# Experts of a two-block network: eleven places for 2 MB weight pieces instead of nine, tokens gathered per group, residual summed in PSUM

## The reference, cut to what matters

```
def ec_moe(x, w_router, w_e_gate, w_e_up, w_e_down):        # x: 1 x 256 x 1024
    cap = CAP_FACTOR * T // N_EXPERTS                       # 32 tokens for each expert
    aff = softmax(x @ w_router)                             # 256 x 16
    g, idx = top_k(aff.transpose(0, 2, 1), cap)
    xs = x[idx]                                             # 16 experts x 32 tokens x 1024
    a = einsum('becd,edf->becf', xs, w_e_gate)              # 16 weights of 1024 x 1024
    u = einsum('becd,edf->becf', xs, w_e_up)
    y = einsum('becf,efd->becd', silu(a) * u, w_e_down) * g
    return zeros(T, D).at[idx].add(y)

x = x + g2 * ec_moe(modulate(rmsnorm(x, norm2), sh2, sc2), ...)
return rmsnorm(x, final_norm)
```

## Time and profile before

| | us |
|---|---|
| median of three runs | 2156.92 |
| lowest, highest | 2155.39, 2157.17 |
| profiled execution, its own time | 2155.87 |
| its span, first to last instruction | 2154.10 |
| PE busy | 1896.1 |
| VectorE busy | 774.6 |
| ACT busy | 523.3 |
| last expert piece used by PE | 2138.10 to 2141.57 |

### The profile page before, as it was taken

One profiled execution on the slowest core, in us unless ns is written; L12 is line 12 of the kernel. 1 busy time (PEld: TensorE's weight loads), 2 busy tenths in 40 slices (PEclk: granted clock), 3 DMA queues, 4 the chain that ended last, 5 costly groups with the idle time before them and its releaser, 6 DMA issues.

```text
span 2154.1 us, 26066 instructions
## 1 busy us (share of the span) xinstructions
PE 1896.1 (88%) x11262; PEld 1434.2 (67%) x11262; DVE 774.6 (36%) x1312; ACT 523.3 (24%) x780; POOL 0.2 (0%) x4
## 2 busy tenths in 40 slices
PE   6999999899998999999999999998999886565555
PEld 5799876799997898766799999545788522111111
DVE  3442332645634433243555675423344300000001
ACT  2201121144431101121244453433352210000000
POOL 0000000000000000000000000000000000000000
PEclk9999999999999999999999999999999998877877
DMA  6221331444442221543644431211025899999996
GB/s 252 98 98 64 152 157 66 189 181 171 173 160 78 90 106 59 210 169 148 242 188 166 177 132 64 78 59 40 1 79 207 349 427 427 428 427 427 427 428 295
DMA packets 30643, 414.13 MB, mean 192 GB/s; under 512 B 3392, under 2 KB 3648, under 8 KB 4288
## 3 DMA queue, kind: packets, MB, share of 16 engines
q1 hardware_dynamic: 29808, 408.69, 47.5%
q10 hardware_dynamic: 720, 3.78, 0.4%
HBM read 411.41 MB, written 1.05 MB: 191 GB/s over the span
## 4 chain that ended last, share of the span: by engine, by line
PE 62%; DMA 18%; DVE 12%; ACT 7%; issue 1%; DVEq 0%; ACTq 0%
PE ps L219 46%; PE ps L751 7%; DMA high<-in_w_e_down_dram 7%; DMA high<-in_w_e_up_dram 6%; DVE rarena L178 4%; ACT rarena L213 4%; DMA high<-in_w_e_gate_dram 4%; PE ps L1141 3%; DVE low L178 3%; PE ps L1503 3%; DVE high L178 2%; ACT high L213 1%; ACT low L213 1%; DVE high L188 1%; PE ps L747 1%
## 5 line engine op out<-in xcount | busy, mean ns | idle before, releaser
L219 PE MATMUL ps<-high,ring 128*128 128x256 f32 (+1 forms) x2016 | 481.9, 390 | 6.3 <-DMA ring<-in_w_in_dram 4.4
L219 PE MATMUL ps<-rarena 128*128 128x256 f32 (+1 forms) x3648 | 457.7, 287 | 7.4 <-DVE rarena L178 7.4
L219 PEld LDWEIGHTS ps<-rarena 128*128 128x128 f32 x3648 | 446.7, 191 | 16.7 <-DVE rarena L178 10.4
L219 PEld LDWEIGHTS ps<-high,ring 128*128 128x128 f32 x2016 | 375.3, 192 | 79.8 <-issue 19.9
L213 ACT ACTIVATE high<-ps 128x512 f32<-128x512 f32 (+2 forms) x210 | 103.2, 492 | 707.3 <-PE ps L1503 275.5
L1503 PE MATMUL ps<-high,low 128*32 128x512 f32 x1040 | 157.1, 733 | 97.5 <-DMA high<-in_w_e_down_dram 35.2
L178 DVE TENSOR_TENSOR rarena<-ring,rarena 128x2048 fp32r<-128x2048 f32 x76 | 167.3, 2201 | 137.5 <-ACT rarena L213 135.8
L213 ACT ACTIVATE rarena<-ring 128x2048 fp32r<-128x2048 f32 x76 | 140.0, 1842 | 149.2 <-DMA ring<-in_w_ffn_up_dram 84.9
L1503 PEld LDWEIGHTS ps<-high,low 128*32 128x32 f32 x1040 | 30.8, 123 | 213.8 <-issue 56.1
L178 DVE TENSOR_TENSOR high<-high,ps 128x512 f32<-128x512 f32 x52 | 35.8, 688 | 314.8 <-PE ps L1503 257.1
L751 PE MATMUL ps<-high 128*128 128x128 f32 (+6 forms) x1024 | 128.8, 298 | 15.3 <-DVE high L178 10.7
(11 more groups left out here) (147 smaller groups left out, 1352.2 us busy)
## 6 DMA issues: line engine op xcount, KB each, us to landing
ring<-in_w_in_dram SPq DMA_DIRECT2D x36, 2048.0 KB, 7.4
ring<-in_w_ffn_up_dram SPq DMA_DIRECT2D x22, 2048.0 KB, 7.5
high<-in_w_e_gate_dram SPq DMA_DIRECT2D x22, 2048.0 KB, 40.7
high<-in_w_e_up_dram SPq DMA_DIRECT2D x22, 2048.0 KB, 41.3
high<-in_w_e_down_dram SPq DMA_DIRECT2D x21, 2048.0 KB, 41.4
ring<-in_w_mod_dram SPq DMA_DIRECT2D x12, 2048.0 KB, 9.3
ring<-in_w_e_down_dram SPq DMA_DIRECT2D x11, 2048.0 KB, 40.6
ring<-in_w_e_gate_dram SPq DMA_DIRECT2D x10, 2048.0 KB, 40.5
```

What stands on the lines that cost most here:

```text
L219: ins = self.e.matmul(out, l, r, start=first and i == 0, stop=end and i == n - 1)
```

## The change

Two more slots (`LOWER`, 9 and 10) are cut from the upper end of the lower arena. In the order of the pieces they stand behind slots 3 and 4 and ahead of the two ring slots that hold the output projection. To make room, buffers of the expert stage are shared or moved: `h2t` lies on `h2` (so ACT waits for the transposes that read the part it writes over), `xs` holds one group's tokens, `hid`, `hT` and `y` are one buffer, the squares use four places instead of eight, `SG` lies over constants that are no longer needed, `fb` over `Sm`, the output over `x`. Tokens are gathered per group, in two batches between the first down steps of the group before. The residual is added by PE: 16 matmuls of `x` with the identity into the combine's open PSUM sums. Squares and the last scaling read PSUM. Turned weights and the row `g2b` are made between the first group's up steps, the row `fb` between the last group's down steps.

```diff
@@ -23,6 +23,7 @@
+LOWER = 2
@@ -287,7 +288,7 @@
-        s_slot = [sem(f"s_slot{i}_landed") for i in range(NSLOT + MORE)]
+        s_slot = [sem(f"s_slot{i}_landed") for i in range(NSLOT + MORE + LOWER)]
@@ -302,6 +303,7 @@
+        slots += [low[:, LOW - (i + 1) * SLOT:LOW - i * SLOT] for i in range(LOWER)]
@@ -535,30 +537,32 @@
-        E.h2t = alloc(2, 1024)
-        E.xs = alloc(8, 512)
-        E.Sm, E.SG = alloc(2, 512), alloc(2, 512)
+        E.h2t = halves(flat(E.h2))
+        E.xs = alloc(8, 128)
+        E.sq = flat(E.xs).rearrange("p (a n) -> p a n", a=4)
...
-        assert place["top"] <= LOW
+        assert place["top"] <= LOW - LOWER * SLOT
...
-        E.SGT = alloc(4, 256)
+        E.Sm = alloc(2, 512)
...
-        E.mx, E.ixu, E.ixf = (E.hid[:, 0, 32 * i:32 * i + 32] for i in range(3))
...
-        E.sq = flat(E.xs)[:, 0:2048].rearrange("p (a n) -> p a n", a=8)
...
-        E.at = flat(E.xs)[:, 2304:2816].rearrange("p (a n) -> p a n", a=2)
-        E.hT = flat(E.Sm).rearrange("p (a n) -> p a n", a=8)
-        E.y4 = halves(flat(E.h2))
-        E.ot = E.y4
-        E.xt = E.h2t
-        E.g2b, E.fb = flat(E.SG), flat(E.bi)
+        top16 = flat(E.hid)
+        E.at = halves(top16[:, 0:512])
+        E.mx, E.ixu, E.ixf = (top16[:, 512 + 32 * i:544 + 32 * i] for i in range(3))
+        E.SG = halves(low[:, top_2 - 256:top_2 + 768])
+        assert coff["e16"][1] >= 768
+        E.SGT = flat(E.bi).rearrange("p (a n) -> p a n", a=4)
+        E.hT = flat(E.hid).rearrange("p (a n) -> p a n", a=8)
+        E.y = flat(E.hid)
+        E.g2b, E.fb = flat(E.SG), flat(E.Sm)
+        E.ot = halves(flat(x))
@@ -705,7 +709,7 @@
-            order = ring_[:1] + [5, 6, 7, 8] + [3, 4] + ring_[1:]
+            order = ring_[:1] + [5, 6, 7, 8] + [3, 4] + [9, 10] + ring_[1:]
@@ -1428,8 +1432,8 @@
-            for t in (1, 0):
-                for hh in range(2):
+            for hh in range(2):
+                for t in range(2):
@@ -1441,7 +1445,7 @@
-            PE.wait_ge("h211", "h210", "h201", "h200")
+            PE.wait_ge("h211")
@@ -1458,10 +1462,13 @@
-            def rest_of_tokens(i):
+            def tokens_of(g_, h):
...
-                b = take_bank(6 + i % 2, f"xs{i}.ps", f"xs{i}")
-                gathered(b[:, 0:384], i, 128, 512).then_inc(*PE(f"xs{i}.ps"))
+                b = take_bank(h, f"xg{g_}{h}.ps", f"xg{g_}{h}")
+                for i in range(4):
+                    ins = gathered(b[:, 128 * i:128 * i + 128], 4 * h + i, 128 * g_, 128 * g_ + 128)
+                ins.then_inc(*PE(f"xg{g_}{h}.ps"))
@@ -1470,29 +1477,28 @@
-                b = take_bank(6 + hh, f"xt{t}{hh}.ps", f"xt{t}{hh}")
-                transposes([(b[:, 128 * i:128 * i + 128], x[:, 4 * hh + i, 128 * t:128 * t + 128])
-                            for i in range(4)]).then_inc(*PE(f"xt{t}{hh}.ps"))
-            def rows(hh):
-                for bank, name, column in ((4, "g2b", lambda i: mod[:, 40 + i, 0:1]),
-                                           (6, "fb", lambda i: pc("final_norm_2", i))):
-                    b = take_bank(bank + hh, f"{name}{hh}.ps", f"{name}{hh}")
-                    for i in range(4):
-                        ins = one(b[:, 128 * i:128 * i + 128], column(4 * hh + i).to_broadcast([128, 128]), ident)
-                    ins.then_inc(*PE(f"{name}{hh}.ps"))
-            between = {("gate", i): (lambda i=i: first_tokens(i + 2)) for i in range(6)}
-            between["gate", 6] = slots_of_tokens
-            for i in range(8):
-                between["up", i] = lambda i=i: rest_of_tokens(i)
-            for t in range(2):
-                between["down", t] = lambda t=t: turned_weights(t)
-                for hh in range(2):
-                    between["down", 2 + 2 * t + hh] = lambda t=t, hh=hh: residual(t, hh)
-            for hh in range(2):
-                between["down", 6 + hh] = lambda hh=hh: rows(hh)
+                for i in range(4):
+                    PE.e.matmul(banks[4 + 2 * t + hh][:, 128 * i:128 * i + 128], x[:, 4 * hh + i, 128 * t:128 * t + 128],
+                                ident, start=False, stop=False)
+            def row(name, bank, hh, column):
+                b = take_bank(bank, f"{name}{hh}.ps", f"{name}{hh}")
+                for i in range(4):
+                    ins = one(b[:, 128 * i:128 * i + 128], column(4 * hh + i).to_broadcast([128, 128]), ident)
+                ins.then_inc(*PE(f"{name}{hh}.ps"))
+            between = {(0, "gate", i): (lambda i=i: first_tokens(i + 2)) for i in range(6)}
+            between[0, "gate", 6] = slots_of_tokens
+            for z in range(2):
+                between[0, "up", 4 + z] = lambda z=z: turned_weights(z)
+                between[0, "up", 6 + z] = lambda z=z: row("g2b", 6 + z, z, lambda i: mod[:, 40 + i, 0:1])
+                for g_ in range(3):
+                    between[g_, "down", z] = lambda g_=g_, z=z: tokens_of(g_ + 1, z)
+                between[3, "down", z] = lambda z=z: row("fb", z, z, lambda i: pc("final_norm_2", i))
+                for t in range(2):
+                    between[1, "gate", 1 + 2 * t + z] = lambda t=t, z=z: residual(t, z)
@@ -1503,8 +1509,8 @@
-                    if g_ == 0 and (nm, k) in between:
-                        between[nm, k]()
+                    if (g_, nm, k) in between:
+                        between[g_, nm, k]()
@@ -1516,16 +1522,14 @@
-                                          E.y4[:, g_ % 2, 512 * ch:512 * ch + 512], start=g_ == 0, stop=g_ == 3)
+                                          E.y[:, 512 * ch:512 * ch + 512], start=g_ == 0, stop=g_ == 3)
...
-                if g_ < 3:
-                    ins.then_inc(*PE(f"comb{g_}"))
...
-                mine = lambda k, e_: E.xs[:, k, 128 * g_ + 32 * e_:128 * g_ + 32 * e_ + 32]
-                if g_ == 1:
-                    PE.wait_ge("xs7")
+                mine = lambda k, e_: E.xs[:, k, 32 * e_:32 * e_ + 32]
+                if g_:
+                    PE.wait_ge(f"xg{g_}1")
@@ -1956,43 +1960,45 @@
-            for t in (1, 0):
+            for t in range(2):
...
-                    A.wait_ge(f"h2{t}{hh}.ps")
+                    A.wait_ge("h210.ps" if (t, hh) == (0, 0) else "h201.ps" if t == 0 else "h211.ps")
...
-            def slots_out(name, i, lo, b):
-                A.wait_ge(f"{name}{i}.ps")
-                A.act(E.xs[:, i, lo:lo + b.shape[1]], b, ACT.Identity, bias=mod[:, 24 + i, 0:1]).then_inc(*A(f"{name}{i}"))
+            def slots_out(i, z):
+                return A.act(E.xs[:, i, :], z, ACT.Identity, bias=mod[:, 24 + i, 0:1])
...
-                slots_out("xs0", i, 0, ps(f"xs0{i}.ps")[:, 0:128])
+                A.wait_ge(f"xs0{i}.ps")
+                slots_out(i, ps(f"xs0{i}.ps")[:, 0:128]).then_inc(*A(f"xs0{i}"))
...
-                A.wait_ge(f"e{g_}gate7.used", f"et{g_ - 1}1.ps" if g_ else "bi2")
+                A.wait_ge(f"e{g_}gate7.used", "bi2")
...
-                    for i in range(8):
-                        slots_out("xs", i, 128, ps(f"xs{i}.ps")[:, 0:384])
...
-                    for t in range(2):
-                        for hh in range(2):
-                            A.wait_ge(f"xt{t}{hh}.ps")
-                            take_copy(E.xt[:, t, 512 * hh:512 * hh + 512], ps(f"xt{t}{hh}.ps")).then_inc(
-                                *A(f"xt{t}{hh}"))
...
-                        for name, dst in (("g2b", E.g2b), ("fb", E.fb)):
-                            A.wait_ge(f"{name}{hh}.ps")
-                            take_copy(dst[:, 512 * hh:512 * hh + 512], ps(f"{name}{hh}.ps")).then_inc(*A(f"{name}{hh}"))
+                        A.wait_ge(f"g2b{hh}.ps")
+                        take_copy(E.g2b[:, 512 * hh:512 * hh + 512], ps(f"g2b{hh}.ps")).then_inc(*A(f"g2b{hh}"))
+                for h in range(2):
+                    if g_ < 3:
+                        A.wait_ge(f"xg{g_ + 1}{h}.ps")
+                        for i in range(4):
+                            ins = slots_out(4 * h + i, ps(f"xg{g_ + 1}{h}.ps")[:, 128 * i:128 * i + 128])
+                            ins.then_inc(*(A(f"xg{g_ + 1}{h}") if i == 3 else A()))
+                    else:
+                        A.wait_ge(f"fb{h}.ps")
+                        take_copy(E.fb[:, 512 * h:512 * h + 512], ps(f"fb{h}.ps")).then_inc(*A(f"fb{h}"))
...
-                    A.wait_ge(f"os{t}{ch}", "et31.ps")
-                    A.act(E.hid[:, ch, :], E.xt[:, t, 512 * ch:512 * ch + 512], ACT.Square,
+                    A.wait_ge(f"acc{t}{ch}")
+                    A.act(flat(E.xs)[:, 512 * ch:512 * ch + 512], banks[4 + 2 * t + ch][:, :], ACT.Square,
@@ -2651,9 +2657,10 @@
-                    V.tt(E.sq[:, i, :], x[:, i, :], x[:, i, :], mul).then_inc(*V())
+                    sq = E.sq[:, i if i < 4 else 1, :]
+                    V.tt(sq, x[:, i, :], x[:, i, :], mul).then_inc(*V())
...
-                        V.tt(E.sq[:, 0, :], E.sq[:, 0, :], E.sq[:, i, :], add).then_inc(*V(f"sq{i}.x"))
```

(19 more changed lines are left out.)

## The result

| | before | changed |
|---|---|---|
| median of five runs, us | 2155.39 | 2144.35 |
| lowest, highest | 2153.98, 2157.17 | 2142.51, 2147.18 |
| profiled execution, us | 2155.87 | 2142.51 |
| its span | 2154.10 | 2140.70 |

The ratio is 0.9949, with a 95% interval of 0.9936 to 0.9963: 11.0 us less (8.0 to 13.8). Forecast was 2146.0 in a range of 2142.6 to 2149.8. Two of the five runs before came after the forecast and lowered that median by 1.5 us, and with it the footing; the difference that was forecast was 10.9 us.

What follows compares the result with a forecast made beforehand. One stream of 96 weight loads sets the end, by its start, its holes and what follows its last landing. Hole 9.7 plus tail 1.2 is 10.9 us off the 2156.92 median: 2146.0, range 2142.6 to 2149.8.

Steps and rivals of the forecast that it cites:

- the hole: Dry stretch of the weight-load stream from 1696, before load 9's bytes: 10.0 us, of which two more slots win 9.7.
- the tail: Work after the last landing, combine to last scaling: without the four adds 1.2 us less, bounds 0.8 and 1.6.
- The rest of the hole: Gap left ahead of load 11, which waits for the first expert step: about 0.3 us instead of 10.0.
- The moved evacuations: ACT's four evacuations of transposed tokens ahead of the first expert step: end 0.75 us later, costed at nothing under 2.0 cover.
- The gathers per group: Tokens gathered in two batches ahead of each of groups 1 to 3, 2.8 us a batch: zero cost, hidden by the stream.
- The first step comes late: Rival, chance 0.10: moved evacuations or PE code fetches delay the first expert step; three us late give 2149.0.
- The hole stays: Rival, chance 0.05: queue takes no tenth and eleventh load ahead, or lower slots come no earlier; only tail won, 2155.7.
- the stream gets slower: Rival, chance 0.03: eleven loads in flight lengthen each load; at 5.10 us for 4.90 the time is 2165.2.
- The tail at half clock: Rival, chance 0.10: the combine after the last expert step runs at half clock, 6.7 us for 3.70, giving 2149.0.
- fixed cost of about 2.0 us of a transfer: Alternative rule for load 11: all 2.0 us ahead of its bytes, starting them at 1707.6, gain 9.2; forecast used 1.46.

Runs made afterwards that it cites:

- e4_late: Changed kernel with four idle 128x512 matmuls ahead of the first expert step; median 2147.95 us, ratio 0.9971 to the kernel before.
- e2_one_low: Changed kernel with one of the two added lower slots in the order, ten slots in all; median 2149.85 us, ratio 0.9985 to the kernel before.
- e9_changed: Changed kernel run again without edits, in a later comparison; median 2145.10 us against 2155.68 before, ratio 0.9947.
- e6_double: Changed kernel with each batch of gathers ahead of groups 1 to 3 done twice; median 2147.48 us, ratio 0.9958 to the kernel before.

## Why the prediction was right

The forecast was 10.9 us of gain, 9.7 from the hole and 1.2 from the tail. Both parts are there in the profiles, at 9.5 and 1.2. That the medians agree to 0.1 us is luck: the interval is 5.8 us wide, the second comparison gave 10.6, and the clock of the tail alone moves an execution of the changed kernel by 3.5 us.

- *The hole* was 10.0 us and closed to 0.9 and 0.3 in two profiles of the changed kernel. Over the profiles the stream takes 486.17 to 486.62 with nine slots and 476.66 to 477.26 with eleven (e4_late left aside, orders as in the changed kernel): 9.5 us between the means, for 9.7. The rest of the hole, which I had put at 0.3 from the end of eleven loads (1653.0 + 53.9) and 1.46 us from issue to bytes, was 0.3 to 0.9. The 1.46 was a simplified reading: it took the bytes to run at full rate from their first moment. In windows of 0.1 us of the kernel before, the first bytes of load 9 come between 1706.5 and 1706.6, 0.9 us behind the issue, and then the rate climbs slowly, as the 197 and 377 GB/s of the earlier trace rows show.
- *The tail* gained 1.22 in the changed kernel and 1.27 alone, for 1.2, inside the bounds of 0.8 and 1.6.
- *The moved evacuations* cost nothing, as costed: the first step starts 51.20 us behind load 0, for 51.41 before. They end 46.66 us behind load 0 for 46.48, 0.2 later and not the 0.75 that I had worked out. The gathers per group cost nothing: a batch is 2.05 us of PE at full clock, less than my 2.8 (two of the six took 3.20, more than that), and doubling them leaves the stream at 476.66. The 0.17 between a PE group and its evacuation held.
- *The first step comes late*: it came no later. Its price was right in size; e4_late shows that 3.2 us at load 11 become 3.0 to 3.6 at the last landing, by the profile of the changed order that one compares with.
- *The hole stays*, *the stream gets slower*: neither. The queue takes eleven loads; the steady rate from 1900 to 2000 is 427 GB/s, for 428.
- *The tail at half clock* is the part that I rated too low. The price for the combine was right in kind, 5.41 (e2_one_low), 6.10 (e9_changed) and 6.14 us (e6_double) for 3.70, where I had 6.7; it was too high because the clock rises before the combine is over. But I gave it a chance of 0.10, and of the nine profiles without idle matmuls in the tail these three have it. The profile before had shown the step at half and the combine at full clock, one case out of several that occur, and I took the combine's level for the usual one. The Trainium skill, TensorE: Matmul & The Clock Gate, "HAM oscillation", had the half clock as the rule for bursts between DMA waits. Its example has longer waits than the up to 3.0 us of idle time ahead of the last steps here, and the runs show both levels. In the two profiles with idle matmuls in the waits all steps behind them are at the upper one, which none of the nine others shows.

The other rule weighed was the fixed cost of about 2.0 us of a transfer (the Trainium skill, DMA: Bandwidth & Descriptors, "Anatomy of one DMA"). That section is about transfers issued from GpSimd, and it puts most of the 2.0 us behind the last byte; the loads here come from the sync queue. With all of it ahead of the bytes the rest of the hole would have been 0.8. The rests that were measured, 0.3 to 0.9, don't decide, but the first bytes do: they came 0.9 us behind the issue, so not all of 2.0 us stands ahead of them here.

## What to carry to other kernels

A stream of loads through a ring of slots is held by two things: its own rate, and the moment at which the first consumer gives a slot back. Divide the time from the stream's start to that moment by the time of one load, and that many slots are needed. Each missing slot costs one load (4.7 and 4.2 us here for the two), and an earlier start only moves the idle time. By this count a twelfth slot would bring no more than the 0.3 to 0.9 us that were left of the hole; no kernel had one. Where executions scatter ahead of the stage by more than the effect, measure the stage from an event at its front to one at its end.

## What the runs showed that was not expected

When the queue is down to one or two loads, the rate can fall although the stream isn't dry. In the changed kernel bytes were still moving when load 11 was issued at 1704.13, and yet the windows from 1704 have 365, 369, 393 and 401 GB/s at a DMA share of 0.88, 1.00, 1.01 and 0.97, until the third load behind it was issued near 1711.6. The second profile of the same kernel has less of it, 410, 397 and 418 GB/s from 1704 to 1710 at 0.96, 1.01 and 1.00. The restart before the change shows it too: 197 GB/s at a share of 0.80. So a busy share of one is not always the full rate. Why the engines are busy at a lower rate there isn't settled by these runs.
